# A two-layer hybrid diffusion trunk: attention pairs with the next scores ahead of both transposes, and the Fourier and norm products in another order

## What is computed

```python
qa = rms_norm(qa.reshape(Bn, L, N_HEADS_A, HEAD_DIM), lp['q_norm'])
ka = rms_norm(ka.reshape(Bn, L, KV_HEADS_A, HEAD_DIM), lp['k_norm'])
if ctx is not None:      # latent: rotary, and cached context keys in the same softmax
    qa = rope_2d(qa)
    k_all = jnp.concatenate([jnp.swapaxes(k_ctx, 1, 2).astype(ka.dtype), rope_2d(ka)], axis=1)
o_a = block_attention(...)              # softmax over blocks of 128 queries
o_b = gate_b * depthwise_conv(gate_c * xb, lp['conv_b_w'])
o_c, s_end = gated_deltanet(...)        # chunked, both directions
o_d = fourier_mix(xd)                   # real part of a 2-D DFT over positions and 64 channels
out = jnp.concatenate([o_a, o_b, o_c, o_d], axis=-1) @ lp['w_out']
```

## Time and profile before

| | |
|---|---|
| median of 3 runs | 3272.24 us (3264.95 to 3273.00) |
| the profiled execution, its time | 3271.25 us |
| the profiled execution, its span | 3269.6 us |
| TensorE busy | 3021.8 us, 92% of the span |
| VectorE busy | 1463.9 us, 45% |
| ScalarE busy | 797.8 us, 24% |
| TensorE's granted clock, mean | 0.944 of full speed |

### The profile page before, as it was taken

One profiled execution on the slowest core, in us unless ns is written; L12 is line 12 of the kernel. 1 busy time (PEld: TensorE's weight loads), 2 busy tenths in 40 slices (PEclk: granted clock), 3 DMA queues, 4 the chain that ended last, 5 costly groups with the idle time before them and its releaser, 6 DMA issues.

```text
span 3269.6 us, 58310 instructions
## 1 busy us (share of the span) xinstructions
PE 3021.8 (92%) x24855; PEld 2838.1 (87%) x24855; DVE 1463.9 (45%) x2396; ACT 797.8 (24%) x1155; POOL 249.2 (8%) x297
## 2 busy tenths in 40 slices
PE   5999999898699989999989999989977988999997
PEld 3999999895488889999989999989846878999997
DVE  3433443515466444334454444452255645344444
ACT  2221121322412232221222222222233223212221
POOL 2000000100022100000010000010001211000001
PEclk6999999998789999999999999989977989999998
DMA  7254322221000133454321122212200002221121
GB/s 244 91 180 154 130 89 77 65 65 52 2 4 3 53 116 130 165 170 134 120 78 59 65 69 77 77 65 78 75 4 3 4 2 78 78 70 65 66 68 45
DMA packets 164006, 259.00 MB, mean 79 GB/s; under 512 B 12892, under 2 KB 131908, under 8 KB 163488
## 3 DMA queue, kind: packets, MB, share of 16 engines
q1 hardware_dynamic: 142112, 174.83, 16.4%
q0 software_dynamic: 21760, 82.20, 7.3%
HBM read 253.85 MB, written 3.15 MB: 79 GB/s over the span
## 4 chain that ended last, share of the span: by engine, by line
PE 67%; issue 24%; DVE 3%; ACT 2%; DMA 1%; POOLq 1%; DVEq 1%; POOL 0%; ACTq 0%
PE ps L562 47%; PE ps L549 16%; PE ps L585 2%; POOLq L447 1%; DMA PT<-mod_w 1%; PE ps L806 1%; DMA ub<-mixer_tables 1%; DVE dTF L1688 0%; DVE PT L1339 0%; ACT pTs L1224 0%; DVEq L1340 0%; DVE pexp L1580 0%; DVE cv L1540 0%; DVEq L1616 0%; DVE xT L1757 0%
## 5 line engine op out<-in xcount | busy, mean ns | idle before, releaser
L562 PE MATMUL ps<-hh,uh 128*128 128x320 f32 x3744 | 865.6, 313 | 58.7 <-DVE hl L1366 48.6
L562 PE MATMUL ps<-hl,uh 128*128 128x320 f32 x3744 | 859.4, 311 | 0.0
L562 PE MATMUL ps<-hh,ul 128*128 128x320 f32 x3744 | 858.3, 311 | 0.0
L562 PEld LDWEIGHTS ps<-hh,uh 128*128 128x128 f32 x3744 | 630.6, 190 | 80.1 <-issue 68.7
L562 PEld LDWEIGHTS ps<-hl,uh 128*128 128x128 f32 x3744 | 632.2, 190 | 0.0
L562 PEld LDWEIGHTS ps<-hh,ul 128*128 128x128 f32 x3744 | 631.6, 189 | 0.0
L1331 DVE TENSOR_TENSOR ul<-raw,uh 128x1024 fp32r<-128x1024 f32 x322 | 390.5, 1234 | 341.2 <-ACT uh L1047 325.6
L1376 DVE SCALAR_TENSOR_TENSOR xT<-ps,modT,xT 128x128 f32<-128x128 f32 x736 | 371.5, 547 | 302.4 <-PE ps L562 301.0
L1047 ACT CAST uh<-raw 128x1024 fp32r<-128x1024 f32 x322 | 323.6, 1046 | 550.8 <-PE ps L562 420.6
L1396 DVE SCALAR_TENSOR_TENSOR PT<-ps,PT 128x640 f32<-128x640 f32 x88 | 72.6, 825 | 689.8 <-PE ps L562 689.8
L562 PE MATMUL ps<-gh,uh 128*128 (+1 forms) x1408 | 325.0, 312 | 15.3 <-DVE ul L1331 14.3
(11 more groups left out here) (236 smaller groups left out, 2406.2 us busy)
## 6 DMA issues: line engine op xcount, KB each, us to landing
raw<-ffn_w SPq DMA_DIRECT2D x264, 512.0 KB
PT<-mod_w POOLq DMA_DIRECT2D x72, 1024.0 KB, 9.2
raw<-w_in SPq DMA_DIRECT2D x40, 512.0 KB
raw<-w_out SPq DMA_DIRECT2D x8, 768.0 KB
ub<-mixer_tables POOLq DMA_DIRECT2D x2, 2176.0 KB, 8.6
out<-PT SPq DMA_DIRECT2D x5, 512.0 KB, 2.6
PT<-x_sample SPq DMA_DIRECT2D x4, 512.0 KB, 6.5
raw<-w_out SPq DMA_DIRECT2D x16, 128.0 KB
```

Of the source, the lines that this page charges most:

```text
L562: last = pe.matmul(pair(q)[:, lo:hi], wt[:, wk * P:(wk + 1) * P], mv(mk, lo, hi), start=start and i == 0 and p_ == 0, stop=stop and i == n ...
```

## The change

In attention, TensorE issues `scores(j+1)` ahead of both turns of pair j, not between them. VectorE scales head 0 of pair j, then does `heads_out(j-1)`, then scales head 1; so the output of a pair is taken out one pair later, and `values` writes bank 6 in place of bank 4. Ahead of attention, the Fourier and norm products come in another order on TensorE, ScalarE and VectorE.

```diff
@@ TensorE
                 fourier_features(0)
+                head_norm_rows(0, 7)
                 pe.wait_ge(ft_in.sem, ft_in.at(l, 16))
                 fourier_tokens(0)
-                head_norm_rows(0, 7)
+                head_norm_spread(0, 7)
                 fourier_features(1)
-                head_norm_spread(0, 7)
-                fourier_tokens(1)
...
                 for n, c in enumerate((C_QA, C_QA + 1, C_KA)):
+                    if n == 2:
+                        pe.wait_ge(f1_used.sem, f1_used.at(l, 2))
                     fp32(bank((2, 3, 6)[n]), tcol(T_ROT), PT[:, c, CTX:T]).then_inc(rot_done.sem, 1)
-                pe.wait_ge(f_lo.sem, f_lo.at(l, 2))
+                fourier_tokens(1)
...
-                    if j and g == 0:
+                    if j and g == 1:
                         pe.wait_ge(pv_used.sem, pv_used.at(l, j))
...
-                            mm = fp32(bank(4, P)[half(g), :], vtok[:, t if j >= 2 else 5, half(g)], pTs[g][:, t, :], t == 0, t == keys[-1])
+                            mm = fp32(bank(6, P)[half(g), :], vtok[:, t if j >= 2 else 5, half(g)], pTs[g][:, t, :], t == 0, t == keys[-1])
...
                 scores(0)
+                pe.wait_ge(f_lo.sem, f_lo.at(l, 2))
                 for j in range(10):
-                    turn(j, 0)
                     if j < 9:
                         scores(j + 1)
+                    turn(j, 0)
                     turn(j, 1)
                     values(j)
@@ ScalarE
-                        fourier_tokens(0)
...
-                fourier_features(1)
+                fourier_tokens(0)
                 act.wait_ge(ob_ready.sem, ob_ready.at(l, 1))
                 act.copy(hh[:, 2:4, :], PT[:, C_GB:C_GB + 2, :]).then_inc(ob_hi.sem, 1)
-                fourier_tokens(1)
+                fourier_features(1)
...
                 act.copy(kall[:, 0:P], bank(1, 128, 256)).then_inc(tr_used.sem, 1)
+                fourier_tokens(1)
@@ VectorE
                     if c:
-                        fourier_lo(0)
+                        ve.wait_ge(nq_ready.sem, nq_ready.at(l, 1))
+                        ve.reciprocal(rrow[0:14, 0, :], rrow[0:14, 1, :]).then_inc(nrow_ready.sem, 1)
...
                 i.then_inc(ob_ready.sem, 1)
-
-
-                ve.wait_ge(nq_ready.sem, nq_ready.at(l, 1))
-                ve.reciprocal(rrow[0:14, 0, :], rrow[0:14, 1, :]).then_inc(nrow_ready.sem, 1)
+                fourier_lo(0)
...
-                fourier_lo(1)
...
                 peaks(0)
+                fourier_lo(1)
                 for j in range(10):
-                    scales(j)
+                    scale(j, 0)
+                    if j:
+                        heads_out(j - 1)
+                    scale(j, 1)
                     if j < 9:
                         peaks(j + 1)
-                    heads_out(j)
+                heads_out(9)
```

More of the change, by code:

```diff
@@ L1571, in peaks, with scale @@
                         ve.tensor_scalar(ast[:, a4 + 1:a4 + 2], ast[:, a4:a4 + 1], -HEAD ** -0.5, None, ALU.mult).then_inc(nmax_ready.sem, 1)
-                def scales(j):
+                def scale(j, g):
                     w = T if j >= 2 else P
-                    for g in range(2):
-                        a4 = 4 * (2 * (j % 2) + g)
-                        ve.wait_ge(p_exp.sem, p_exp.at(l, 2 * j + g + 1))
-                        ve.reciprocal(ast[:, a4 + 3:a4 + 4], ast[:, a4 + 2:a4 + 3])
-                        ve.drain()
-                        ve.tensor_scalar(pexp[j % 2][:, g, 0:w], pexp[j % 2][:, g, 0:w], ast[:, a4 + 3:a4 + 4], None, ALU.mult).then_inc(p_ready.sem, 1)
+                    a4 = 4 * (2 * (j % 2) + g)
+                    ve.wait_ge(p_exp.sem, p_exp.at(l, 2 * j + g + 1))
+                    ve.reciprocal(ast[:, a4 + 3:a4 + 4], ast[:, a4 + 2:a4 + 3])
+                    ve.drain()
+                    ve.tensor_scalar(pexp[j % 2][:, g, 0:w], pexp[j % 2][:, g, 0:w], ast[:, a4 + 3:a4 + 4], None, ALU.mult).then_inc(p_ready.sem, 1)
                 def heads_out(j):
@@ L1585, in heads_out @@
                     hs = hh[:, c, n * P:(n + 1) * P]
-                    ve.tensor_copy(hs, bank(4, P))
+                    ve.tensor_copy(hs, bank(6, P))
                     ve.drain()
-                    ve.tensor_tensor(hl[:, c, n * P:(n + 1) * P], bank(4, P), hs.bitcast(F32), ALU.subtract).then_inc(pv_used.sem, 1)
+                    ve.tensor_tensor(hl[:, c, n * P:(n + 1) * P], bank(6, P), hs.bitcast(F32), ALU.subtract).then_inc(pv_used.sem, 1)
                 peaks(0)
+                fourier_lo(1)
                 for j in range(10):
-                    scales(j)
+                    scale(j, 0)
+                    if j:
+                        heads_out(j - 1)
+                    scale(j, 1)
                     if j < 9:
                         peaks(j + 1)
-                    heads_out(j)
+                heads_out(9)
                 ve.tensor_scalar(PS[32:40, :], PS[32:40, :], adt[32:40, 1:2], None, ALU.add).then_inc(sp_x.sem, 1)
```

## The result

The changed kernel takes 3230.56 us (median of 4 runs, 3223.85 to 3234.0); the kernel before took 3271.61 beside it (median of 4, 3264.95 to 3273.0). The ratio is 0.9877, with a 95% interval of 0.9858 to 0.9895: 1.2% faster, 41 us.

A forecast was written before the change was run, and what follows sets the result against it. TensorE, busy 92% of the span, was taken as the bound, with engines waiting for each other in the attention pairs. Savings of 21.6 + 5.6 + 2.0 = 29.2 us gave 3243.0 us against the median; range 3232 to 3258.

The forecast's parts named there:

- Large rounds: Attention, pair 2 to pair 9: rounds of 5.09 us instead of 6.29, saving 21.6 us over both layers.
- the wait that the change removes: Attention pairs: TensorE stands still 1.46 us ahead of each first turn, until VectorE's scaling releases it.
- One more fall of the clock 1.7: Ahead of attention, second tokens: one clock fall costing 1.7 us, putting the first exponential at 819.7.
- One round at the lower level: Attention, seven large rounds a layer: one at the lower clock, 7.38 us, and six at the upper, 5.09 each.
- Pairs 0 and 1: Start of attention, first exponential of pair 0 to pair 2: 1.6 us saved a layer, between zero and two times 1.20.
- The end: End of attention, after the exponentials of pair 9: 1.2 us saved a layer, between 0 and 2.5.
- What follows attention is untouched and starts earlier: Everything behind attention: no change of its own forecast, only an earlier start.
- Ahead of attention: From the projection to the first exponential: 1.0 us saved a layer, 2.0 together, bounds +2.5 and -2.8.
- A: Norm's rows stay at the lower clock behind the 6.2 us gap, taking 15.4 us, not 9.4: 3255, chance 0.12.
- B: Attention pairs: the clock keeps falling twice a layer, each fall costing 1.6 us: 3249.4, chance 0.15.
- C: Attention: the round closes through `heads_out` and the next maxima, so it shortens little, to 5.94 us: 3263, chance 0.07.
- D: Slower: the 6.2 us gap lowers the clock and nothing before the output product raises it: 29 us lost, 3301, chance 0.06.

The follow-up runs named there:

- e1: The kernel before with only the pair loop's changes, everything ahead of the first scores left as before: 3238.81 us, ratio 0.9894.
- e7: The changed kernel with the first copy of each pair's output done five times on VectorE: 3254.45 us, single run.
- e9: The changed kernel with the first copy of each pair's output done six times on VectorE: 3264.04 us, single run.
- e6: The changed kernel with the first copy of each pair's output done twice on VectorE: 3237.69 us, single run.
- e8: The changed kernel with the norm's spread contracted over 128 rows, not 14, and an early 8-element exponential on ScalarE to load its table: 3229.02 us.
- e10: e8 with the broadcasts of the DeltaNet stage contracted over 128 rows in place of 8: 3205.52 us.

## Why the prediction was right in kind and wrong in size

**Large rounds: right.** 5.04 us measured, 5.09 forecast, and the wait that the change removes was the one named. The chain has lost VectorE, e1 shows the round with the pair loop alone, and e7 measures the spare time at 0.60 where 0.6 was worked out.

**The clock: charged too often.** This is the step that failed: the prediction assumed that a fall stands where a fall stood before. That assumption sits in three of the four terms that came out too small, and in part of the fourth. (1) "One more fall of the clock 1.7" was charged to the second tokens of each layer. They took 7.48 us, at the upper level. With 0.5 us that the transposes and rotary products came sooner, the first exponential is at 817.37 (820.92 - 3.55), not 819.7: 2.3 us in layer 0. (2) One round at the lower level in each layer was priced at 7.38; it took 7.16 in layer 0 and 6.48 in layer 1. Together with six rounds 0.05 shorter in each layer, that is the 1.8 us between 21.6 and 23.4. (3) Pairs 0 and 1 saved 2.36 us a layer, at the upper bound named, 2 x 1.20, not 1.6. This term was held down for another reason, that pair 0 has no output to pass. In e1, whose first scores still ran at 0.50 (818 to 824), these pairs saved 1.92, so 0.3 of the miss lay in the waits; the other 0.44 came with the order ahead of attention, which raised the granted clock of this stretch from 0.50 (819.5 to 829.4) to 0.69 (820 to 829). (4) The end was given 1.2 a layer and saved 2.61 and 1.66. Before, in layer 0, the ten last transposes took 2.40 us and the last values ran at the lower level too (0.50 from 884 to 887.5), as the prediction's upper bound of 2.5 had it; now the two last turns take 0.77 each and the values 1.31. The four come to 7.7 us, 36.9 against 29.2.

**Untouched stretches: no place in the range.** The other 4 us of the 12 between forecast and median are no term of the change. Among the profiled executions the time to the first projection's end goes from 753.9 to 758.5 us, and the DeltaNet stage, with the same code, from 186 to 193. "What follows attention is untouched and starts earlier" is right as to work. But the range was made of the bounds of the edited parts alone; that such steps also stand between a profiled execution and a median was left out. Its low end stood for a gain of 40 us (29.2 + 11), and 41 came. Whether part of the gain in the DeltaNet stage is an effect of attention's order on the clock behind it is open: layer 0 lost 2.67 us there and layer 1 gained 4.96.

**Ahead of attention: right step by step.** The gap ahead of the norm's rows was forecast at 6.2 and is 6.30; the rows 9.4 and 9.52; the third chunk at 789.3 and 789.03 (792.58 - 3.55); the transposes, released by the cached values, at 804.8 and 804.5.

**The rivals.** A, rows of 15.4 us behind the gap: they took 9.52. B, falls that keep coming: none in the rounds from pair 3 on. In the windows of after the granted clock is 1.00 from 836 to 870, with ten transposes in one block in each round. The Trainium skill, page TensorE: Matmul & The Clock Gate, Part 4: PE-mode transpose, says that the full rate doesn't engage for transposes; this trace does not bear it out, since the block takes 1.31 us, where ten transposes at the lower level took 2.40 before. The argument for B was sound in one thing: rounds with longer waits do fall back, as e9 shows. C, a ring through `heads_out`: excluded by e6, where a copy more does not lengthen a steady round. D, slower: excluded by the clock in nearly all rounds. The table load that is now on the path costs 1.28 us, from its start at 819.63 to the exponential at 820.92. The Trainium skill, page ScalarE: Activation LUTs, section What ACT_TABLE_LOAD costs, has 2.66 with the drain; by an estimate from it the load would cost 1.4 more a layer. No such time stands between the two rows.

## What to carry to other kernels

When a wait is taken out of a ring that sits at the edge of TensorE's clock level, count the clock too: look for rounds of two lengths in the profile before, and price the gain once with the falls gone and once with them kept. Here nearly all of them went. If an engine is ringed by three others, find whether one of two edits is enough: here putting independent scores ahead of a turn hid the same VectorE work as reordering VectorE did. And give the range the spread of the stretches that the change does not touch.

## What the hardware showed that was not expected

TensorE can be busy without a gap and still run at its lower level, 1.2 GHz, when its products contract over few rows: 0.51 over 9.4 us of unbroken work with 14 rows, 1.00 with 128 rows in the same place and behind a wait as long (1.39 against 1.19 us), 10.88 against 5.92 us for twenty products. It can even fall there: in the kernel before, within the unbroken row of 28 such products, the granted clock was 1.00 from 787.1 to 789.2 and 0.50 from 789.2 on. The 8-row broadcasts of the DeltaNet stage took 7.16 us for 32, hardly more than the 6.74 with 128 rows, yet with them changed the granted clock over 100 us of that stage rose from 0.93 to 1.00, and the kernel went from 3229.02 to 3205.52 us. Letting these products contract over all rows, with zeros in the table for the added ones, was the largest gain of all the edits tried after the change. In the spread, and between e8 and e10, the number of rows is all that differs. How the chip takes such products into account is not settled by these runs.
